# Two transformer blocks on one core: where the squares of the residual stream are taken, and in which order the second group of a feed-forward stage is begun

## The reference

```python
def rms_norm(x, g):
    xf = x.astype(jnp.float32)
    y = xf * lax.rsqrt(jnp.mean(xf * xf, axis=-1, keepdims=True) + EPS)
    return (y * g.astype(jnp.float32)).astype(x.dtype)

def swiglu(h, w_gate, w_up, w_down):
    return (jax.nn.silu(h @ w_gate) * (h @ w_up)) @ w_down

x = x + 0.5 * rms_norm(f, g[5])          # f: result of a feed-forward part on rms_norm(x, g[4])

h = h + jnp.square(jax.nn.relu(hn @ w_ff1[l])) @ w_ff2[l]     # second block
```

## Time and profile before

| | |
|---|---|
| runs | 1531.38, 1531.5 and 1532.52 us, median 1531.5 us |
| profiled execution | 1529.18 us, span of its trace 1527.4 us |
| TensorE matmuls busy | 1410.1 us |
| TensorE weight loads busy (beside the matmuls) | 1150.4 us |
| DVE busy | 837.1 us |
| ACT busy | 683.8 us |
| POOL busy | 49.5 us |
| mean granted TensorE clock | 0.962 |
| DMA | 247.10 MB, 162 GB/s in the mean |
| chain of waits that ended last | PE 83%, DVE 8%, ACT 5%, issue 2%, POOL 1% |

### The profile page before, as it was taken

One profiled execution on the slowest core, in us unless ns is written; L12 is line 12 of the kernel. 1 busy time (PEld: TensorE's weight loads), 2 busy tenths in 40 slices (PEclk: granted clock), 3 DMA queues, 4 the chain that ended last, 5 costly groups with the idle time before them and its releaser, 6 DMA issues.

```text
span 1527.4 us, 17343 instructions
## 1 busy us (share of the span) xinstructions
PE 1410.1 (92%) x6508; PEld 1150.4 (75%) x6508; DVE 837.1 (55%) x956; ACT 683.8 (45%) x868; POOL 49.5 (3%) x95
## 2 busy tenths in 40 slices
PE   5999999589999999999966899999999968999997
PEld 4888878478888787888854678887787647778886
DVE  4455565664555655545658554556667165655553
ACT  4344454343444544443455444345663164354442
POOL 1000010010000100000010000000000000000000
PEclk9999999799999999999997999999999977999999
DMA  7555646155556455555530255565643311455550
GB/s 257 166 191 187 213 157 227 35 163 176 190 180 233 146 185 165 184 184 192 210 138 1 83 184 186 191 209 166 221 165 123 128 56 56 165 188 172 191 179 28
DMA packets 160157, 247.10 MB, mean 162 GB/s; under 512 B 9006, under 2 KB 104424, under 8 KB 160104
## 3 DMA queue, kind: packets, MB, share of 16 engines
q1 hardware_dynamic: 159824, 246.28, 48.5%
q10 hardware_dynamic: 280, 0.10, 0.0%
HBM read 245.30 MB, written 1.05 MB: 161 GB/s over the span
## 4 chain that ended last, share of the span: by engine, by line
PE 83%; DVE 8%; ACT 5%; issue 2%; POOL 1%; DMA 0%; ACTq 0%; POOLq 0%; DVEq 0%
PE GU L484 15%; PE GU L486 15%; PE GU L485 15%; PE DD L484 10%; PE DD L486 10%; PE DD L485 10%; DVE wlo L1453 2%; ACT whi L1052 2%; PE TB L520 2%; PE TB L654 2%; ACT xh L1064 1%; DVE xl L1468 1%; PE DD L895 1%; DVE sm L1691 1%; ACT junk L1072 1%
## 5 line engine op out<-in xcount | busy, mean ns | idle before, releaser
L1453 DVE TENSOR_TENSOR wlo<-raw,whi 128x2048 fp32r<-128x2048 f32 (+1 forms) x226 | 512.9, 2282 | 273.1 <-ACT whi L1052 273.1
L1052 ACT ACTIVATE whi<-raw 128x2048 fp32r<-128x2048 f32 (+1 forms) x226 | 429.1, 1909 | 172.5 <-PE DD L486 169.9
L484 PE MATMUL GU<-whi,xh 128*128 128x512 f32 (+1 forms) x1088 | 435.4, 400 | 23.5 <-DVE hid L1566 11.5
L485 PE MATMUL GU<-wlo,xh 128*128 128x512 f32 (+1 forms) x1088 | 427.2, 393 | 0.0
L486 PE MATMUL GU<-whi,xl 128*128 128x512 f32 (+1 forms) x1088 | 427.2, 393 | 0.0
L484 PEld LDWEIGHTS GU<-whi,xh 128*128 128x128 f32 x1088 | 207.5, 191 | 71.9 <-issue 17.6
L486 PEld LDWEIGHTS GU<-whi,xl 128*128 128x128 f32 x1088 | 207.3, 191 | 44.2
L485 PEld LDWEIGHTS GU<-wlo,xh 128*128 128x128 f32 x1088 | 207.6, 191 | 40.4
L484 PE MATMUL DD<-whi,hth 128*128 128x512 f32 x480 | 188.4, 393 | 0.0
L486 PE MATMUL DD<-whi,htl 128*128 128x512 f32 x480 | 186.9, 389 | 0.0
L485 PE MATMUL DD<-wlo,hth 128*128 128x512 f32 x480 | 186.8, 389 | 0.0
(11 more groups left out here) (253 smaller groups left out, 963.2 us busy)
## 6 DMA issues: line engine op xcount, KB each, us to landing
raw<-in_w_ffn_gate SPq DMA_DIRECT2D x88, 512.0 KB, 4.0
raw<-in_w_ffn_up SPq DMA_DIRECT2D x88, 512.0 KB, 4.9
raw<-in_w_ffn_down SPq DMA_DIRECT2D x88, 512.0 KB, 4.3
raw<-in_w_ff SPq DMA_DIRECT2D x64, 512.0 KB, 4.3
raw<-in_w_in SPq DMA_DIRECT2D x40, 512.0 KB, 4.6
raw<-in_w_conv_in SPq DMA_DIRECT2D x24, 512.0 KB, 4.9
raw<-in_w_kv SPq DMA_DIRECT2D x16, 512.0 KB, 4.8
raw<-in_w_conv_out SPq DMA_DIRECT2D x8, 512.0 KB, 4.7
```

Source lines behind the costliest of these rows:

```text
L484: pe.matmul(dst, h, w_h, start=start, stop=False)
L485: pe.matmul(dst, h, w_l, start=False, stop=False)
L1052: nc.scalar.activation(whi[s][:, 0:size], raw[s][:, 0:size], ACT.Copy).then_inc(hi_done[s], 1)
L1453: nc.vector.tensor_tensor(wlo[s][:, 0:size], raw[s][:, 0:size], whi[s][:, 0:size].bitcast(F32), ALU.subtract).then_inc(lo_done[s], 1)
```

## The change

Five things change.

1. A list `SQUARES` gives the order in which ACT takes the sums and POOL works them off; it runs by row half (post of half 0, pre of half 0, post of half 1, pre of half 1) where `NORMS` had each norm's two halves together. All waits for `ssq_ready` and `rs_ready` take their count from it.
2. On ACT the squares of `x` half 0 are taken ahead of `xh` of half 0, for all entries and for all four tails.
3. In `enter` on ACT, the squares of `x` half 1 stand between the two banks of `xh` of half 1. Where a post norm comes first, the split of the third weight block is moved ahead of these banks.
4. On DVE, at the entry of a feed-forward stage, `hid` of half 0 in group 0 is multiplied between the `wlo` of the third block and that of the fourth.
5. On TensorE, group 1 of a feed-forward stage does the first block by rows: wait for bank 0, 12 matmuls of half 0, wait for bank 1, 12 of half 1.

```diff
+        SQUARES = [("pre0", 0), ("pre0", 1)]
+        for i, name in enumerate(("pre1", "pre2", "pre3", "pre5", "pre6", "pre7")):
+            for t in range(TT):
+                SQUARES += [(f"post{i}", t), (name, t)]
+        SQUARES += [("pre8", 0), ("pre8", 1), ("final", 0), ("final", 1)]
+
+        def order(name, t=1):
+
+            return SQUARES.index(("pre3" if name == "pre4" else name, t)) + 1
...
-                order = [(k, t) for t in range(TT) for k in range(4)] if last else \
-                        [(k, t) for k in range(4) for t in range(TT)]
-                for i, (k, t) in enumerate(order):
+                seq = [(k, t) for t in range(TT) for k in range(4)] if last or rows else \
+                      [(k, t) for k in range(4) for t in range(TT)]
+                for i, (k, t) in enumerate(seq):
...
-                    if read and i < 2 and read[1]:
+                    if read and k == 0 and read[1]:
                         pe.wait_ge(read[0][t], read[1])
...
-                    for t in range(TT):
-                        pe.wait_ge(gu_used[t], d + gu0 + g)
-                    x_half(gu_banks, es[0], 0, 0, False, d=d)
+                    if g == 1:
+                        x_half(gu_banks, es[0], 0, 0, False, read=(gu_used, gu0 + 1), rows=True)
+                    else:
+                        for t in range(TT):
+                            pe.wait_ge(gu_used[t], d + gu0 + g)
+                        x_half(gu_banks, es[0], 0, 0, False, d=d)
...
                 if i is not None:
                     post_sq(i, 1, last)
-                for b in range(2):
-                    prep_bank(PRE[pre], 1, b)
-                split_to(seg[then] + 3)
+                    split_to(seg[then] + 3)
+                prep_bank(PRE[pre], 1, 0)
                 if pre != "pre4":
                     if n.x:
                         act.wait_ge(x_ready, 4 * n.x)
-                    sumsq(pre, 0)
+                    sumsq(pre, 1)
+                prep_bank(PRE[pre], 1, 1)
                 split_to(seg[then] + 4)
-                if pre != "pre4":
-                    sumsq(pre, 1)
...
                     split_to(seg[then] + 2)
+                    act.wait_ge(x_ready, 4 * (n.x - 1) + 2)
+                    sumsq(pre_next, 0)
                     for b in range(2):
                         prep_bank(PRE[pre_next], 0, b)
                     enter(pre_next, then, last, i)
...
-                dve.wait_ge(rs_ready, ncol[name] + 2)
+                dve.wait_ge(rs_ready, order(name))
...
-                split_to(seg[then] + 4)
+                split_to(seg[then] + (3 if then[:2] == "ff" else 4))
...
+                dve.wait_ge(rs_ready, order(pre))
+                hidden_rows(0, 0, 0)
                 split_to(base + 4)
-                dve.wait_ge(rs_ready, ncol[pre] + 2)
-                hidden(0, 0)
+                hidden_rows(0, 1, 0)
...
             def norms(first, last):
-                for name in NORMS[NORMS.index(first):NORMS.index(last) + 1]:
-                    for t in range(TT):
-                        c = ncol[name] + t
-                        pool.wait_ge(ssq_ready, c + 1)
-                        norm(1, ssq[:, c:c + 1], msq[:, c:c + 1], rs[:, c:c + 1], D, rs_ready)
+                for i in range(order(first, 0) - 1, order(last)):
+                    c = ncol[SQUARES[i][0]] + SQUARES[i][1]
+                    pool.wait_ge(ssq_ready, i + 1)
+                    norm(1, ssq[:, c:c + 1], msq[:, c:c + 1], rs[:, c:c + 1], D, rs_ready)
```

More of the change, by code:

```diff
@@ L486, in mm3, with x_half @@
                 return pe.matmul(dst, l, w_h, start=False, stop=stop)
-            def x_half(dst, e, half, first_k, last, d=0, done=None, read=None):
+            def x_half(dst, e, half, first_k, last, d=0, done=None, read=None, rows=False):
                 s, m = e.slot, e.cols
@@ L1071, in sumsq @@
                 n.ssq += 1
+                assert n.ssq == order(name, t)
                 nc.scalar.activation(junk[:, :], x[:, t, :], ACT.Square, accum_out=ssq[:, c:c + 1]).then_inc(ssq_ready, 1)
@@ L1082, in post_sq @@
                 n.ssq += 1
+                assert n.ssq == order(f"post{i}", t)
                 nc.scalar.activation(junk[:, :], DD[:, 2 * t:2 * t + 2, :].rearrange("p a n -> p (a n)"),
@@ L1110, in after_rows @@
                 split_to(seg[then] + 2)
+                act.wait_ge(x_ready, 4 * (n.x - 1) + 2)
+                sumsq(pre, 0)
                 for b in range(2):
@@ L1127, in evacuate @@
                     if g == 0:
-                        act.wait_ge(rs_ready, ncol[name] + 2)
+                        act.wait_ge(rs_ready, order(name))
                         if scale is not None:
@@ L1183, in ffn @@
                 split_to(base + 4)
-                act.wait_ge(rs_ready, ncol[pre] + 2)
+                act.wait_ge(rs_ready, order(pre))
                 gate(0, 0)
@@ L1282, in group @@
                     if g == 0:
-                        act.wait_ge(rs_ready, ncol["pre7"] + 2)
+                        act.wait_ge(rs_ready, order("pre7"))
                     m = ent[seg["w_in"] + 2 * g].cols
@@ L1408, in _ @@
             split_to(2)
+            sumsq("pre0", 0)
             enter("pre0", "ffn0", None)
@@ L1476, in post_tmp @@
                     dve.wait_ge(gain_loaded[i % 2], 16 * (i // 2 + 1))
-                dve.wait_ge(ssq_ready, ncol[f"post{i}"] + t + 1)
+                dve.wait_ge(ssq_ready, order(f"post{i}", t))
                 for nn in range(2):
@@ L1485, in post_x @@
                 if nn == 0:
-                    dve.wait_ge(rs_ready, ncol[f"post{i}"] + t + 1)
+                    dve.wait_ge(rs_ready, order(f"post{i}", t))
                     dve.wait_ge(d_used[t], n.d)
@@ L1755, in dve_final @@
                 for t in range(TT):
-                    dve.wait_ge(rs_ready, ncol["final"] + t + 1)
+                    dve.wait_ge(rs_ready, order("final", t))
                     nc.vector.scalar_tensor_tensor(out=tmp[:, t, :], in0=x[:, t, :], scalar=rcol("final", t),
@@ L1786, in group @@
                         split_to(seg["w_in"] + 2 * (g + 2) + 2)
-                dve.wait_ge(rs_ready, ncol["pre7"] + 2)
+                dve.wait_ge(rs_ready, order("pre7"))
                 for g in range(3):
@@ L2145, in _ @@
             norms("pre0", "pre5")
-            pool.wait_ge(rs_ready, ncol["pre5"] + 2)
+            pool.wait_ge(rs_ready, order("pre5"))
             nc.gpsimd.tensor_scalar(r8[:, :], rs[:, ncol["pre5"]:ncol["pre5"] + 2], 0.125, None, ALU.mult).then_inc(r8_ready, 1)
```

## The result

| Kernel | Median us | Lowest to highest | Runs | Profiled execution: time, span |
|---|---|---|---|---|
| before | 1531.44 | 1531.21 to 1532.52 | 4 | 1529.18, 1527.4 |
| changed | 1517.03 | 1514.76 to 1517.27 | 4 | 1516.87, 1515.1 |

The ratio is 0.9901, with a 95% interval of 0.9884 to 0.9918: the changed kernel is 14.4 us faster by the medians, 12.3 by the spans of the two profiled executions. The forecast was 1515.5, with a range of 1510 to 1521.

A forecast was written before the change was run, and what follows sets the result against it. TensorE was taken to set the end, losing time only in holes and half-clock stretches. Holes 14.08 plus clock 6.01 less tails 4.12 gave 15.97 us gained: 1531.5 - 16.0 = 1515.5 us, range 1510 to 1521.

The forecast's parts named there:

- parts 1 and 2: Feed-forward entries: early Square and split, DVE's new order and TensorE by rows close holes worth 14.08 of 15.40 us.
- The spare of 1.0 us at half 0: ffn1, group 1: `hid` of half 0 done at 339.2, TensorE due at 340.14, so the hole of 3.59 closes whole.
- 1.32 predicted: ffn0's entry: ACT's table load still stands ahead of Silu, so 1.32 us of hole stay and 2.17 go.
- None of the waits changed its name: Sign of failure at the entries: TensorE's wait would change from `hid` to `wlo`.
- the rival of holes closed in part: Entries: each hole keeps 1.32 us, as ffn0 does; gain 10.7, time 1520.8 us; chance 0.14.
- 6.01 us were to come back: Entries of ffn0, ffn1 and ff: half-clock time after the holes goes, 2.87 + 1.57 + 1.57 us.
- That ffn0's fall would go: ffn0's entry: no clock fall behind the 1.32 us that stay, 2.87 us back; bounds 0 and 2.87.
- 4 x 1.03 = 4.12 predicted: Four tails, ffn0 to ffn3: Square between `whi` and `xh` on ACT delays the transposes by 1.03 us each.
- The small new wait for `xl`: Sign at the four tails: a small new TensorE wait for `xl` at the head's first matmuls; no size given.
- The rivals with 0 and with 2 x 1.03 a tail: Four tails: Square hidden, 1511.4 us, chance 0.12; or both Squares show, 8.2 us, with clock falls 1534.0, chance 0.02.
- The Square of half 0 at an entry: ffn1, ffn3 and ff: fits ACT's 1.18 us of idle time ahead of `xh`; at ffn0 ACT is idle; cost 0.
- the clock elsewhere: Attention and mixer stages: shifted waits meet other clock moments, 1.57 to 2.87 us per fall; two or more falls: chance 0.07.

The follow-up runs named there:

- squares-alone kernel: Changed kernel, but TensorE takes group 1 in the old order, waiting for both banks, and DVE makes both `hid` behind both `wlo`: 1524.75 us, ratio 0.9949.
- rows-alone kernel: Kernel before, with only TensorE's group 1 by rows and DVE's `hid` of half 0 ahead of the fourth block's `wlo`; Squares unmoved: 1523.12 us, ratio 0.9935.
- before 2: Second profiled execution of the kernel before, with no edit: median 1532.89 us, span 1531.1.

## Why the prediction was right

**The holes.** All five came out by the steps of parts 1 and 2. From `xh` of half 1 on, the sum put the Square at +1.01, the second bank at +2.04, the split at +3.05, Silu at +4.86, `hid` of half 0 done at +7.04 and of half 1 at +9.74; the profile has +1.02, +2.06, +3.06, +4.86, +6.97 and +9.56. The spare of 1.0 us at half 0 is 1.04 (336.39 - 335.35). At ff ACT frees the bank at 1336.17 against 1336.76, 0.6 as predicted. At ffn0 1.4 us of hole stay, 1.32 predicted. None of the waits changed its name; the rival of holes closed in part fell.

**The clock at the entries.** 6.01 us were to come back, and all five windows are at 1.00. With the holes that is 20.1 predicted and 20.5 measured. That ffn0's fall would go rested on one row, that of ffn2; it held in all four executions. It was less safe than it looked, though: the squares-alone kernel has a hole of 2.5 us there and the rows-alone kernel one of 2.4, and both ran slow matmuls behind it. The 6.01 was also read from a single execution: in `before 2` the five entries take 1.3 us more (50.5 against 49.2), all of it in the clock. That the price came out so well has a part of luck.

**The tails.** 4 x 1.03 = 4.12 predicted, 4.1 measured, and moving the two lines gave it back. The small new wait for `xl` that was foretold is 0.2 us; 0.5 more stands under `issue`. The rivals with 0 and with 2 x 1.03 a tail both fell; that the second Square, between the banks of half 1, lies behind other work is shown by the same 1.03.

**The Square of half 0 at an entry** cost nothing, as predicted: it ran while ACT waited for the transposes.

**POOL.** The working took 1.25 us for the last `msq`, the only value gave; in the changed kernel it is 0.19, since no `wlo` runs there. It didn't matter, because rs had 0.8 us to spare by that value. It did for the rows alone: the step that failed there was to take a duration along into an order in which its neighbour was gone.

**The sum.** 1531.5 - 16.0 = 1515.5 against 1517.03. The steps that the change touches give -16.4 in the ledger; the medians differ by 14.4. What is left, 2 us (4.2 in the first pair of profiles), is the rival called "the clock elsewhere", which came in beside the forecast in a small dose. Conv stage, attention and mixers together took 501.2 and 503.4 us in the two executions of before, and 505.4, 503.4, 505.8 and 506.6 in the four of after: a mean of +3.0. The forecast set this at zero. In the squares-alone and rows-alone kernels and the three executions with the tail Square behind `xh` and no filler the three stretches take 502.5 to 504.4, between the means of 502.3 for before and 505.3 for after. Whether the changed kernel's later work really meets the clock worse, or four and two executions only fell so, stays open; the runs of the changed kernel with a mean granted clock of 0.970 spent less time at the lower level than any run of before (at most 0.962).

**The better version.** The changed kernel with its tail Square behind `xh` and the table load early took 1508.4 to 1508.5 us twice, 8.6 less than the 1517.03 of the changed kernel's first runs and 5.6 less than the 1514.03 of the later ones. The tails and ffn0's entry account for 4.1 + 1.4 = 5.5. The rest of the 8.6 is the difference between the two sets of runs of the changed kernel.

## What to carry to other kernels

When an engine waits at the joint of two groups, write down all instructions that its releaser's engine has queued in front, with their durations, and lay them out anew in the new order: six durations from one timeline gave every restart here to 0.2 us. Ask of each work that is moved earlier which other chain it now stands in: the same Square was free where ACT waited for transposes and cost its full 1.03 us where the chain ran through ACT without a pause. And read a small operation's duration together with what ran beside it on its neighbour engine before it is carried into another order.

## What the runs showed of the hardware

- POOL's operation on 128x1 takes 0.19 us alone and up to 1.65 (the longest of its 30 in the profile after) when it starts under a DVE subtraction of two SBUF operands: it ends 0.05 us after that one, in all 128 cases of the twelve profiles.
- The granted clock after one and the same hole differs from execution to execution: ffn3's 3.5 us in the kernel before was followed by 1.00 once, by 0.68 once. Over all holes at the entries, by starts: the eight of 3.2 to 3.6 us were followed by the lower level seven times, the three of 2.4 to 2.5 us in the two half kernels each time, and the thirteen of 1.0 to 2.0 us never.
- The times of the changed kernel spread more than those of the kernel before: 1507.6 to 1519.3 against 1530.9 to 1534.7. They go with the mean granted clock, 0.960 to 0.970 against 0.957 to 0.962. Why isn't known; the version with the tail's Square and the table load moved, which has no hole at the entries either, took 1506.6 to 1510.7 in ten runs, about the spread of before.
- 12 filler matmuls ahead of the output projection and those in the attention kept TensorE at full speed for the next 32 matmuls, 2.3 us, and no longer than to its next wait.
